# First feed-forward matrix as seven products of quarters, feed-forward in three passes, low parts of its weights all on POOL

## What is computed

```python
# block 1, layer l; mod is a product of a vector with ada_w[l] (1024 x 6144)
h = rmsnorm(x, norm_ffn_g[l]) * (1.0 + sc2) + sh2
f = (jax.nn.silu(h @ ffn_w1[l]) * (h @ ffn_w3[l])) @ ffn_w2[l]
x = x + g2 * f
# block 2: gate, up = split(x @ w_ffn_in[i]); ffn = (silu(gate) * up) @ w_ffn_out[i]
```

## Time and profile before

| | before |
|---|---|
| median of 3 runs | 2618.8 us |
| profiled execution: first to last instruction | 2610.1 us |
| around that span, median less span | 8.7 us |
| PE busy | 2489.1 us, 95% |
| DVE / ACT / POOL busy | 41% / 34% / 41% |
| granted TensorE clock, mean | 0.976 |
| read from HBM | 264.51 MB, 102 GB/s |

### The profile page before, as it was taken

The page is one execution under the profiler, slowest core; times in us unless marked ns, Lnnn a source line. Parts: engine busy times, 40 slices in busy tenths (PEclk is TensorE's granted clock), DMA queues, the critical chain, the costliest instruction groups (busy, mean ns, idle before and its releaser), DMA issues.

```text
span 2610.1 us, 30256 instructions
## 1 busy us (share of the span) xinstructions
PE 2489.1 (95%) x11670; PEld 1993.8 (76%) x11670; DVE 1070.5 (41%) x1718; ACT 884.0 (34%) x1153; POOL 1075.8 (41%) x373
## 2 busy tenths in 40 slices
PE   7799999999999999999999999999989998999997
PEld 4576788878777788888787678888769776888875
DVE  5798520069477640000496440000247746000014
ACT  4225422222425422222443542222233354222222
POOL 0334255544234055553253435554424533555442
PEclk8899999999899999999999999999999999999998
DMA  7513432267322433323321213222332211222231
GB/s 276 178 55 119 149 97 93 90 206 223 99 81 81 161 97 97 96 78 99 99 79 59 65 65 97 96 96 83 99 91 81 73 49 65 97 96 96 88 93 61
DMA packets 297044, 267.89 MB, mean 103 GB/s; under 512 B 20104, under 2 KB 273784, under 8 KB 296696
## 3 DMA queue, kind: packets, MB, share of 16 engines
q1 hardware_dynamic: 296952, 266.63, 32.5%
HBM read 264.51 MB, written 2.10 MB: 102 GB/s over the span
## 4 chain that ended last, share of the span: by engine, by line
PE 80%; DVE 9%; issue 6%; ACT 2%; POOL 2%; DMA 1%; SPq 0%; DVEq 0%; ACTq 0%; POOLq 0%
PE bank L2361 25%; PE bank L2363 24%; PE bank L2362 24%; DVE m_cv L1828 2%; POOL w_lo L1351 1%; PE bank L2896 1%; DVE g_acc L1588 1%; ACT w_hi L817 1%; PE bank L2814 1%; PE bank L2929 1%; PE bank L2608 1%; DVE small L1714 0%; PE bank L2863 0%; DVE a_acc L1588 0%; DVE n_qi L2165 0%
## 5 line engine op out<-in xcount | busy, mean ns | idle before, releaser
L1351 POOL TENSOR_TENSOR w_lo<-raw,w_hi 128x2048 fp32r<-128x2048 f32 (+1 forms) x201 | 849.3, 4225 | 1179.1 <-ACT w_hi L817 1152.3
L2361 PE MATMUL bank<-h_hi,w_lo 128*128 128x512 f32 (+1 forms) x2192 | 871.3, 398 | 50.3 <-DVE h_lo L1695 22.7
L2362 PE MATMUL bank<-h_lo,w_hi 128*128 128x512 f32 (+1 forms) x2192 | 860.2, 392 | 0.0
L2363 PE MATMUL bank<-h_hi,w_hi 128*128 128x512 f32 (+1 forms) x2192 | 859.9, 392 | 0.0
L2361 PEld LDWEIGHTS bank<-h_hi,w_lo 128*128 128x128 f32 (+1 forms) x2192 | 415.6, 190 | 155.0 <-issue 61.9
L817 ACT ACTIVATE w_hi<-raw 128x2048 fp32r<-128x2048 f32 (+1 forms) x216 | 378.3, 1751 | 444.4 <-PE bank L2363 417.0
L2362 PEld LDWEIGHTS bank<-h_lo,w_hi 128*128 128x128 f32 (+1 forms) x2192 | 415.6, 190 | 89.0 <-issue 3.0
L2363 PEld LDWEIGHTS bank<-h_hi,w_hi 128*128 128x128 f32 (+1 forms) x2192 | 414.9, 189 | 89.2 <-issue 0.4
L1738 DVE TENSOR_TENSOR f_full<-f_act,bank 128x512 f32<-128x512 f32 x88 | 60.5, 687 | 840.0 <-PE bank L2363 840.0
L2361 PE MATMUL bank<-f_hi,w_lo 128*128 128x512 f32 x704 | 280.4, 398 | 2.4 <-POOL w_lo L1351 2.4
L2363 PE MATMUL bank<-f_hi,w_hi 128*128 128x512 f32 x704 | 278.8, 396 | 0.0
(11 more groups left out here) (356 smaller groups left out, 2315.7 us busy)
## 6 DMA issues: line engine op xcount, KB each, us to landing
raw<-in_ffn_w SPq DMA_DIRECT2D x44, 1024.0 KB
raw<-in_w_ffn_in SPq DMA_DIRECT2D x44, 1024.0 KB
raw<-in_w_in SPq DMA_DIRECT2D x34, 1024.0 KB
raw<-in_ffn_w SPq DMA_DIRECT2D x32, 704.0 KB
raw<-in_w_ffn_out SPq DMA_DIRECT2D x32, 704.0 KB
b_raw<-in_ada_w SPq DMA_DIRECT2D x16, 1024.0 KB, 8.0
a_raw<-in_ada_w SPq DMA_DIRECT2D x32, 512.0 KB, 4.7
z_a<-in_ada_w SPq DMA_DIRECT2D x4, 2048.0 KB, 14.3
```

The lines of the kernel that those rows point to most:

```text
L1351: pool.tensor_tensor(b.w_lo[p][:, 0:n], b.raw[p][:, 0:n], b.w_hi[p][:, 0:n].bitcast(F32), ALU.subtract)\
L2361: pe.matmul(out, wlo, xhi, start=start, stop=False)
L2362: pe.matmul(out, whi, xlo, start=False, stop=False)
L2363: return pe.matmul(out, whi, xhi, start=False, stop=stop)
```

## The change

**Seven products.** For a 256-column piece of w1, the 8 row tiles are taken as even and odd ones and the 2 column tiles as left and right: four quarters of 512 x 128. The input h is cut likewise, even and odd tiles by left and right 256 tokens. The piece's product is made of seven products of 4 steps, 12 matmuls with 256 moving columns each (84 in place of 48 with 512). Three of them (M1, M2, M3) move h itself; four (M6, M7, M5, M4) move sums of quarters of h, `t_hi` and `t_lo`, made once for each feed-forward. Three need sums of weight quarters, four `tensor_tensor` on DVE for each piece (`dve_sums`). DVE puts the output together with five operations (`parts`). w3 keeps its 48 matmuls ("plain").

**Three passes.** Pairs 0 to 3, 4 to 7 and 8 to 10 are each followed by their share of w2, in four "down" units of two output tiles, which DVE adds to x three times in all. The units are 34 for each feed-forward: 0 to 9 pairs 0 to 4, 10 to 13 down, 14 to 21 pairs 5 to 8, 22 to 25 down, 26 to 29 pairs 9 and 10, 30 to 33 down. Everything is written out, without the loops of before.

**A ring.** High and low weights lie in a ring of 8 slots of 128 x 512, one for each product of a seven, two of 8 tiles of a plain unit or a pair of a down unit: 165 for each feed-forward. ACT may fill a slot when the product eight before is done, and POOL makes every low part.

**Modulation.** The next layer's comes in 16 pieces of 1 MB through one buffer, one behind each of the units 12 to 27; PE folds after every second one. SP waits for each sum before it issues the next piece, in its queue of weights. The buffers of `b_late` become two of their own and two that lie elsewhere, and its four pieces stand behind units 1, 2, 4 and 5.

```diff
+class Plan:
...
+        for n, pairs in enumerate(PASSES):
+            upto = min(pairs[-1] + 2, PAIRS)
+            for i in range(done, upto):
+                self.units += [("seven", i, 0), ("plain", i, 0)]
+            done = upto
+            self.units += [("down", n, j) for j in range(KD // 2)]
...
+    def on_vector(self, u, n):
+        kind = self.units[u][0]
+        return False
...
+def sp_next_modulation(sp, e, l, n):
...
+    if n:
+        sp.wait_ge(*s.a_acc(l, KD // 2 * n))
+    sp.dma_start(e.b.b_raw[3][:, :, :],
...
+    for t, (u, part) in enumerate(plan.seq):
+        if part == 0 and u and plan.units[u - 1][0] == "plain":
+            hidden(plan.units[u - 1][1])
+        for q in plan.after[t]:
+            pool_low(pool, e, lay, q)
...
+def dve_sums(dve, e, lay, u):
...
+    dve.tensor_tensor(s1, a21, a22, ALU.add).then_inc(s.f_sum.up, 1)
+    dve.wait_ge(*s.f_sum(n, 4 * i + 1))
+    dve.tensor_tensor(s2, s1, a11, ALU.subtract).then_inc(s.f_sum.up, 1)
+    dve.tensor_tensor(a21, a11, a21, ALU.subtract).then_inc(s.f_sum.up, 1)
+    dve.wait_ge(*s.f_sum(n, 4 * i + 2))
+    dve.tensor_tensor(s4, a12, s2, ALU.subtract).then_inc(s.f_sum.up, 1)
...
+    def after(u):
+        if u in (1, 2, 4, 5):
+            if u == 4:
+                dve.wait_ge(*s.b_pe(l, 2))
+            weigh_b({1: 4, 2: 5, 4: 6, 5: 7}[u])
...
+        if more and 12 <= u < 12 + A_CHUNKS:
+            dve_next_modulation(dve, e, l, u - 12)
...
+    def seven(u, i, parts):
+        for part in parts:
+            at, v = AREA[part]
+            pe.wait_ge(*s.low_in(n, plan, plan.at[u, part]))
+            if i == 0 and part in (M6, M7, M5, M4):
+                pe.wait_ge(*(s.t1_l(lay.l, {M6: 5, M7: 6, M5: 7, M4: 8}[part]) if plan.early else s.t2_l(lay.l, 4)))
+            for k in range(4):
+                op = product(bank[at][:, v], u, part, k, start=(part in (M1, M7, M5, M2) and k == 0),
+                             stop=(part in (M6, M7, M4, M3) and k == 3))
...
+        if l + 1 < DEPTH and 14 <= u < 14 + A_CHUNKS and u % 2 == 0:
+            i = (u - 14) // 2
+            fold(bank[MOD_BANK[0]], b.r, range(4 * i, 4 * i + 4), s.a_acc(l, KD * (i + 1))).then_inc(s.a_fold.up, 1)
```

More of the change, by code:

```diff
@@ L35 @@
 FF = 2816
-KF = FF // P
 DEPTH = 2
@@ L645, in sp_parameters, with sp_ffn, sp_after_ffn @@
+def sp_ffn(sp, e, lay, w1, w3, c3, w2, l, first=0, between=None):
+    for u in range(first, len(lay.plan.units)):
+        sp_ffn_unit(sp, e, lay, u, w1, w3, c3, w2, l)
+        if between is not None:
+            between(u)
+def sp_after_ffn(sp, e, n):
+    plan, s = PLAN[1 + n // DEPTH], e.s
+    sp.wait_ge(*s.low_in(n, plan, PRODUCTS - 1))
 def sp_parameters(sp, e, l):
@@ L886, in act_next, with act_high @@
-def act_next(act, e, lay, p):
+def act_high(act, e, lay, q):
+    s, b, plan, n = e.s, e.b, lay.plan, lay.ffn
+    u, part = plan.seq[q]
+    kind, i, _ = plan.units[u]
+    if q >= RING:
+        act.wait_ge(*s.f_step(n, plan.before[q] + 1))
+    else:
+        act.wait_ge(*s.slot_free(lay.ffn_pair, q // 4))
+    if kind == "seven" and part in (M5, M6, M7, M3):
+        act.wait_ge(*s.f_sum(n, 4 * i + {M5: 1, M6: 2, M7: 3, M3: 4}[part]))
+    else:
+        act.wait_ge(*s.f_in[u % 2](n, 16 * (u // 2 + 1)))
+    src, hi, _ = stationary(b, lay.blk, plan, q)
+    act.activation(hi, src, ACT.Copy).then_inc(s.f_hi.up, 1)
@@ L1292, in act_layer2 @@
     act_layer_norm(act, e, l)
+    for t in range(4):
+        act.wait_ge(*s.t2_d(l, t + 1))
+        act.activation(b.t_hi[:, t, :, :], b.t_raw[:, t, :, :], ACT.Copy).then_inc(s.t2_h.up, 1)
     for k in range(KD):
@@ L1734, in body @@
         for m in range(2):
[L1735 to L1737 removed]
+            dve.wait_ge(*s.f_silu(n, 2 * i + (1 if m else 2)))
             dve.tensor_tensor(b.f_full[:, m, :], b.f_act[:, m, :], bank[2 + m][:, :], ALU.mult)\
[L1739 to L1744 removed]
@@ L1745, in dve_ffn @@
-    with dve.Fori(0 if between is None else 2, 11) as i:
-        body(i)
+               .then_inc(s.f_gated.up, 1)
+    for t, (u, part) in enumerate(plan.seq):
+        kind, i, j = plan.units[u]
+        last = t == plan.end(u)
+        if u >= plan.tail:
+            break
+        if kind == "seven":
+            parts(u, i, part)
+        if part == (M7 if plan.early and u == 0 else M5) and u + 2 < plan.tail and plan.units[u + 2][0] == "seven":
+            dve_sums(dve, e, lay, u + 2)
+        if kind == "plain" and last and not (plan.early and u == 1):
+            gated(u, i)
+        if plan.early and (u, part) == (0, M4):
+            gated(1, 0)
+        if kind == "down" and last:
+            for m in range(2):
+                down(u, 2 * j + m, m)
+        for q in plan.after[t - 1] if t else ():
+            if plan.mine[q]:
+                dve_low_part(dve, e, lay, q)
+        if last and after is not None:
+            after(u)
@@ L1749, in dve_layer1, with dve_tile_in @@
+def dve_tile_in(dve, e, lay, u, m):
+    s, plan, n = e.s, lay.plan, lay.ffn
+    if m == 0:
+        dve.wait_ge(*s.f_tile(n, sum(x[0] == "down" for x in plan.units[:u + 1])))
+    else:
+        dve.wait_ge(*s.f_step(n, plan.end(u) + 1))
 def dve_layer1(dve, e, l, more):
@@ L2100, in dve_shift_norm @@
         shift(k)
-    for k in range(1, 5):
+    for k in range(1, 4):
         dve.wait_ge(*s.n2_d(l, k + 1))
@@ L2516, in pe_layer1 @@
     lay = Layer(s, 1, l)
-    def add_partitions(part, first, last):
-        half = A_CHUNKS // 2
-        pe.wait_ge(*s.a_acc(l - 1, KD * half * (part + 1)))
-        for n in range(2 * half * part + first, 2 * half * part + last):
-            op = pe.matmul(bank[MOD_BANK[part]][:, n:n + 1], b.a_acc[:, n * P:(n + 1) * P], b.ones[:, 0:1],
-                           start=True, stop=True)
-        if last == 2 * half:
-            op.then_inc(s.a_pe.up, 1)
     def project(i):
```

786 lines of the change are left out of this document (498 added, 288 removed).

## The result

The changed kernel takes 2625.85 us (median of 19 runs, 2621.13 to 2629.29); the kernel before, measured again beside it, 2617.04 (19 runs, 2607.9 to 2621.83). The ratio over all runs is 1.0038, 95% interval 1.0029 to 1.0047 (the two medians alone give 1.0034): about 0.4% or 10 us slower. The profiled execution has a span of 2624.0 us, against 2610.1. These spans are 13.9 us apart, more than the 10, because the execution profiled before was one of the quicker ones of its kernel (a span of 2610.1 where the median time is 2617.04), while the one profiled after is its kernel's median.

The account below looks back on a forecast made before the run. PE, on 80% of the chain that ended last, was taken as the bound. Terms -29 - 6.4 + 18 + 10 + 2 + 10 + 2 = +6.6 on the span of 2610.1 gave 2616.7, with 8.7 more 2625 us; range 2590 to 2662.

Parts of the forecast that it names:

- Matmuls, -29: Pieces of w1: seven products of short matmuls save PE time over 44 pieces, -29 us (ends -36 and -22).
- slow matmuls on the sums of h: Sevens: 48 matmuls moving `t_hi` and `t_lo` might each pay 6.6 ns, so a piece saves only 0.50 us, 22 in all.
- Next modulation, +18: First feed-forward, units 12 to 27: PE waits for DVE's sums at every second unit, +18 us (ends 0 and +33).
- rival B: Modulation links fit: sums under 5.4 us, weight sums meet POOL's gaps, starts at half, full matmul pace; 2595 us, chance 0.34.
- Starts of block 1, +10: Block 1's two feed-forward starts: PE waits before M6 and unit 2, sums late behind modulation piece 4; +10 us (0; +16).
- Boundary of the layers, -13.4: Between layers 1 and 2 of block 1: 6.8 us of waiting, 3.48 of folds and 3.1 of low clock go, -13.4 us.
- folds, +7: First feed-forward: the 64 modulation folds, at 0.109 us each, come back inside it, +7 us.
- Block 2's gates, +2: Start of block 2's feed-forward: both banks must be free, sums of h fit behind the gate; +2 us (0; +4).
- Ends of block 2, +10: Block 2's feed-forward ends: last tile taken some 3 us late, 7 in the first layer; together +10 us (+4; +14).
- POOL and DVE in the steady stretch, 0: Pairs of units: POOL's 18.6 us and DVE's 6.8 to 10.8 fit into PE's 21.1, so 0 us.
- Rival D: POOL the bound everywhere: each of its 13 operations for a pair costs 1.7 us, +44 on the sum; 2669 us, chance 0.08.
- A's time: Case as summed: the product saves, the queues take a little more; 2625 us, between 2615 and 2635, chance 0.37.

Follow-up runs that it names:

- Runs 4: Changed kernel, with DVE adding only one of four rows of each piece of the next layer's modulation (work left out): 1.0030 to the kernel before.
- 7: Kernel before the change, with DVE adding only one of four rows of each piece of the next layer's modulation: 0.9992 to the unedited kernel before.
- Run 2: Changed kernel, with modulation pieces 4 to 7 summed one unit later in block 1 and their first fold behind unit 4: 1.0106 to the kernel before.
- runs 5: Changed kernel, with unit 2's weights in block 1 loaded early into memory of their own: 1.0023 to the kernel before.
- 10: Changed kernel, with unit 2's weights loaded early and modulation piece 4 summed behind unit 0's last parts: 1.0024 to the kernel before.
- Run 3: Changed kernel, with POOL splitting block 2's last two pairs of gate weights before the low parts of the sums of h: 1.0026 to the kernel before.
- run 8: Changed kernel, with the low parts of w2 weights made on DVE, not POOL, in the first two passes: 1.0042 to the kernel before.

## Why the prediction was right in sum and wrong in its terms

Forecast 2625.0, range 2590 to 2662, slower the likeliest; measured 2625.85. On the spans I had +6.6 and it was +13.9. The sign holds, and roughly the size. That the number fits to a microsecond is luck, twice over. Several terms were wrong and cancelled. And the 8.7 us that I put between span and median are not time around the span: every recorded execution takes 1.7 to 1.9 us longer than its own span, and the rest of the 8.7 is how far the execution profiled before lay below the median. With 1.9 the sum would have read 2618.6, and the change in the runs, 10 us, lies between my +6.6 and the +13.9 of the two profiles.

- **Matmuls, -29: too small.** 0.90 us a piece, -40. The term I had put in between, slow matmuls on the sums of h because they lie near f_hi, is refuted: they run at 0.1179, faster than those on h (0.120).
- **Next modulation, +18: wrong in whole.** Runs 4 and 7 put it at 0 (3.3 us of sums after, 3.4 before). The failed step is "beside a seven that is 2.6 + 4 sums (6.8 in turns), longer than the landing". A sum of a piece did take 6.5 us, as I had it. But I let every weight sum wait for POOL, where two of four found a gap, and I let DVE's work of the unit stand in the link to its full length, though it runs while the piece lands. A link was (625.8 - 449.6) / 15 = 11.7 us, within my 8.2 to 12.0, or 23.5 for two; the folds stood 22.7 us apart on the mean, and the first sums were 3.3 us ahead of theirs. That was rival B's mechanism in its second half, the gaps; its first, a sum under 5.4 us, did not hold where units are pairs (5.8 to 6.6).
- **Starts of block 1, +10: too small by far.** With the sevens' -10 and the folds' +7 taken out of the table, block 1's feed-forwards lost 12.9 + 10 - 7 = 15.9 and 7.8 + 10 = 17.8, and ends are 1 each in them by the prediction. 10.3 and 10.2 are the stall, 2.7 and 1.9 the clock behind it, 2.3 and 3.1 the two short waits before M6 that I had forecast at 3, 2.9 and 0.8 the fold that came late, with its clock; 3.4 and 1.0 us of waits for low parts fell away. That leaves nothing in the first layer and some 2 us in the second that I can't place. The failed step is the one that named piece 4 of the modulation as what makes the sums late. I never followed the load: that unit 2's buffer is freed by low parts whose slots come free only at the end of units 0 and 1, and that 5.5 us of landing then stand in the row. Run 2 shows that the named cause was not the last, runs 5 and 10 that it was the next behind the load, and the chain of run 10 that the loop of low parts and load comes back one pair of units later. What binds behind all of them stays open.
- **Boundary of the layers, -13.4, and folds, +7.** Measured -6.6 for the whole stretch between the feed-forwards. 2.6 us of the shortfall lie in the mixer, where PE waits 5.5 and not 2.9 us for `mf` on ACT; that wait changes between kernels whose edits don't touch it, so I don't lay it to the change. The first product stood 12.1 us behind the last update of x before and 7.6 after: 4.5 us and not the 6.8 that I had taken from the other boundary. The folds of 3.48 us went as forecast. The clock did not come back in whole: it is still 0.74 over 684.7 to 689.7, behind the first product.
- **Block 2's gates, +2: too small.** +4.6 and +7.0. The low parts of the sums of h stand ahead of a split on POOL; I had counted only the sums on DVE. Run 3 shows the mechanism: it takes back 1.8 of the 4.6 and 1.4 of the 7.0, and the rest then stands behind DVE's part. In the second layer some 2 us lie ahead of the gate, 1.1 of them right behind the last w2 tile, where the two sums now stand: the next operation on x starts 6.0 us behind the last update, 4.9 before.
- **Ends of block 2, +10.** The feed-forwards gave -4.4 and -8.7 with -10 each from the sevens, so ends cost some 6 and 1. PE's waits are the forecast ones, smaller: 3.8 + 1.3 us in the first layer, where POOL's split of the next weights falls on a square sum, and 1.3 in the second.
- **POOL and DVE in the steady stretch, 0: right.** PE's only waits for low parts of these weights are 2.4 us at the two starts, POOL is 55% busy (forecast 60), its short operations take 1.43 us on the mean, and run 8, for the w2 units, changes nothing. Rival D is out. The code without its loops shows as no wait either: PE's waits that end with nothing visible are 2.9 us in all, two of 0.8 more than before, both ahead of block 2's feed-forwards. The rule of the Trainium skill that I had cited ("SBUF — State Buffer", section "Who interferes with whom") is borne out by 1.66 to 1.78 us for weight sums that take 0.69 alone; what it leaves open is how often the two meet, and that decided the modulation's term.

In short: A's time with B's modulation, and with starts and gates worse than in either.

## What to carry to other kernels

When units are reordered at the start of a stage, follow the buffer and not only the queue: what frees it, when, and how long the next load takes once it is free. A stall behind such a loop costs its length and then the low clock. Taking one load out of the loop halved the stall here and gave 4 us, since the same loop closed again around the next one: read the chain anew after each edit, at the new place where the engine stands.

A single chain of "load, add, load" that is about as long as the stage (23.5 us against 22.7 for a pair) cost one wait of 1.5 us here; ask what else the engine can do while the load lands before adding it to the link.

## What the runs showed of the hardware

- Matmuls of 256 columns came at 0.1179 and 0.120 us, those of 512 at 0.2267 to 0.2333, all at full clock. Half the columns cost 51 to 53%.
- The pace of matmuls whose moved tile lies in f_hi or f_lo depends on where the region begins: 0.2333 us at 128672 and 128768, 0.2287 at 128704. The short ones on the sums of h, in the same region, came at 0.1179, 0.1188 and 0.1178 in this order; those on h, whose tiles didn't move, kept theirs. Nothing in the runs says why.
- PE stood for 10.3 us and came back at a clock of 0.50; it was at 1.00 again about 6 us after its first matmul, which cost 2.7 us. It stood for 1.5 us at the third fold and was at full pace at first, then seven matmuls long at the lower level, which cost 1.4.
